# Last projection of a two-block transformer kernel: eight plain weight tiles against seven products with tokens as rows

## What is computed

```python
def second_block(x, ...):
    ...
        a = (a * jax.nn.silu(za)) @ w_att_out[l]
        ...
        sgo = (sgo * jax.nn.silu(zs)) @ w_sg_out[l]
        ga, gs = jnp.split(jax.nn.sigmoid(gm + b_merge[l]), N_BRANCHES, axis=-1)
        y = ga * a + gs * sgo
        x = x + y @ w_o[l]
    return rmsnorm_2(x, final_g)      # row mean of squares, 1/sqrt, times final_g
```

## Time and profile before

| what | us |
|---|---|
| median of 3 runs (1296.0 to 1296.04) | 1296.03 |
| the profiled execution's own time | 1295.99 |
| its span, from first to last recorded event | 1294.2 |
| TensorE busy (share of the span) | 1287.6 (99%) |
| VectorE busy | 818.7 (63%) |
| ScalarE busy | 622.6 (48%) |
| GpSimd busy | 703.7 (54%) |

### The profile page before, as it was taken

The page is one execution under the profiler, slowest core; times in us unless marked ns, Lnnn a source line. Parts: engine busy times, 40 slices in busy tenths (PEclk is TensorE's granted clock), DMA queues, the critical chain, the costliest instruction groups (busy, mean ns, idle before and its releaser), DMA issues.

```text
span 1294.2 us, 20065 instructions
## 1 busy us (share of the span) xinstructions
PE 1287.6 (99%) x7784; PEld 1116.6 (86%) x7784; DVE 818.7 (63%) x1253; ACT 622.6 (48%) x1004; POOL 703.7 (54%) x504
## 2 busy tenths in 40 slices
...
DMA packets 143626, 127.10 MB, mean 98 GB/s; under 512 B 4464, under 2 KB 138736, under 8 KB 143536
## 3 DMA queue, kind: packets, MB, share of 16 engines
...
## 4 chain that ended last, share of the span: by engine, by line
PE 99%; DMA 1%; ACT 0%; DVE 0%; issue 0%; SPq 0%; ACTq 0%
PE gemm L813 17%; PE gemm L814 17%; PE gemm L821 16%; PE gemm L1125 9%; PE gemm L1130 9%; PE gemm L1126 9%; PE gemm L870 2%; PE gemm L871 2%; PE gemm L876 2%; PE gemm L837 2%; PE gemm L838 2%; PE gemm L843 2%; PE mix L1251 1%; PE mix L1239 1%; PE mix L1228 1%; DMA xtm<-x 1%
## 5 line engine op out<-in xcount | busy, mean ns | idle before, releaser
L678 POOL TENSOR_TENSOR wlo<-raw,whi 128x512 fp32r<-128x512 f32 x280 | 388.2, 1419 | 307.3 <-ACT whi L1415 287.8
L813 PE MATMUL gemm<-hh,whi 128*128 128x512 f32 x584 | 232.1, 397 | 0.0
L814 PE MATMUL gemm<-hl,whi 128*128 128x512 f32 x584 | 227.8, 390 | 0.0
L706 POOL TENSOR_TENSOR wlo<-raw,whi 128x512 fp32r<-128x512 f32 x108 | 159.5, 1503 | 47.0 <-ACT whi L1624 41.6
L1415 ACT ACTIVATE whi<-raw 128x2048 fp32r<-128x2048 f32 x66 | 126.1, 1910 | 45.2 <-PE gemm L821 26.1
L821 PE MATMUL gemm<-hh,wlo 128*128 128x512 f32 x584 | 145.9, 390 | 0.0
L813 PEld LDWEIGHTS gemm<-hh,whi 128*128 128x128 f32 x584 | 109.7, 188 | 26.7 <-issue 4.0
L814 PEld LDWEIGHTS gemm<-hl,whi 128*128 128x128 f32 x584 | 109.8, 188 | 22.0 <-issue 0.2
L821 PEld LDWEIGHTS gemm<-hh,wlo 128*128 128x128 f32 x584 | 109.2, 188 | 22.4
L1125 PE MATMUL gemm<-hh,whi 128*128 128x256 f32 x496 | 124.7, 284 | 0.0
L1126 PE MATMUL gemm<-hl,whi 128*128 128x256 f32 x496 | 124.3, 283 | 0.0
...
## 6 DMA issues: line engine op xcount, KB each, us to landing
...
```

Source lines behind the costliest of these rows:

```text
L678: last = nc.gpsimd.tensor_tensor(a(wlo), a(raw), as_f32(a(whi)), ALU.subtract)
L706: return nc.gpsimd.tensor_tensor(part_of(wlo, u, b), raw_block(u, f, k), as_f32(part_of(whi, u, b)), sub)
L813: mm(bank[:, :], w, xh[:, k, :], start=(k == 0), stop=False)
L814: mm(bank[:, :], w, xl[:, k, :], start=False, stop=False)
```

## The change

The weights `w_o2` are cut into quadrants of 512 x 512: `wa[0]`, `wa[1]` are the upper k-half (feature columns 0 to 511 and 512 to 1023), `wb[0]`, `wb[1]` the lower. `y2` is cut into left and right tokens (256 each) and k-blocks 0 to 3 and 4 to 7. Seven quadrant products take the place of eight. In each, 128 tokens are the loaded operand and 512 weight columns stream, so results come out with tokens as rows and are added to rows of the residual, `xr[t]`. Those rows are made by 32 transposes of `xT` between the tiles of the `w_so` product, copied by ACT. The combinations are: sums of `y2` quadrants (`u_sum`, DVE), sums of weight quadrants (`w_sum` by DVE, `wa[1]` by POOL), their high parts (ACT) and rests (DVE, POOL), and sums of products afterwards. The order of products is P1, P2 (plain), P5, P6, P7 (of sums), P3, P4. Squares are summed along rows by ACT, and `fg2` becomes a broadcast row `fg2b`, loaded by DMA.

The diff, cut. Removed throughout are the units of `w_o2`, `turn_out`, `last_tile`, `turn_half`, `row_sum`, `last_rows`, `last_sum`, `square_out`, `copy_out` and the old `row_out`.

```diff
+sp.wait_ge(sem("mixed_ps"), KD)
+for f in range(2):
+    sp.dma_start(wa[f][:, :, :], cols(w_o2, f * 512, 512, 0, 4)).then_inc(sem("wT_in"), 16)
+for i, f in enumerate((1, 0)):
+    slot_free(n_o2 + i)
+    load(n_o2 + i, cols(w_o2, f * 512, 512, 4, 4), wb[f])
+sp.wait_ge(sem("y2_sum"), KD)
+sp.dma_start(fg2b[:, :], fg2_row.partition_broadcast(P)).then_inc(sem("c2_in"), 16)
+for t, h, done, count in ((2, 0, "out_dve", 1), (2, 1, "out_act", 1), (3, 0, "out_dve", 2), (3, 1, "out_act", 2),
+                          (0, 1, "out_dve", 3), (0, 0, "out_dve", 4), (1, 0, "out_act", 3), (1, 1, "out_dve", 5)):
+    sp.wait_ge(sem(done), count)
+    sp.dma_start(out[t * P:(t + 1) * P, h * 512:(h + 1) * 512], xr[t][:, h * 512:(h + 1) * 512]).then_inc(sem("o_out"), 16)
...
+def block_rest(i, block):
+    high, low = W_SLOT[LAST_SLOT[i]]
+    pool.wait_ge(sem("hi_done"), N_UNITS + i + 1)
+    for k in range(4):
+        last = nc.gpsimd.tensor_tensor(low[:, k, :], block[:, k, :], as_f32(high[:, k, :]), sub)
+    last.then_inc(sem("lo_done"), 1)
+block_rest(L_P1, wa[0])
+block_rest(L_P2, wb[0])
+pool.wait_ge(sem("s_made"), 3 * N_SEVEN + 1)
+for k in range(4):
+    last = nc.gpsimd.tensor_tensor(wa[1][:, k, :], wa[0][:, k, :], wa[1][:, k, :], sub)
+last.then_inc(sem("s3_made"), 1)
+pool.wait_ge(sem("o_copied"), 8)
+for t in range(2):
+    pool.wait_ge(sem("p1_read"), N_SEVEN + 1 + t)
+    o = xr[t][:, 0:512]
+    nc.gpsimd.tensor_tensor(o, o, p1_s(t), ALU.add).then_inc(sem("row_pre"), 1)
+block_rest(L_P7, wa[1])
+for t in range(2):
+    pool.wait_ge(sem("p1_read"), N_SEVEN + 3 + t)
+    o = xr[2 + t][:, 0:512]
+    nc.gpsimd.tensor_tensor(o, o, p5_s(t), ALU.add).then_inc(sem("row_pre"), 1)
+    pool.wait_ge(sem("row_pre"), 3 + 2 * t)
+    nc.gpsimd.tensor_tensor(p5_s(t), p5_s(t), xr[2 + t][:, 512:], ALU.add).then_inc(sem("row_pre"), 1)
+block_rest(L_P4, wb[1])
+pool.wait_ge(sem("c2_in"), 80)
+for t, h, count in ((2, 1, 3), (3, 1, 4), (1, 0, 2)):
+    pool.wait_ge(sem("row_sq"), count)
+    o = xr[t][:, h * 512:(h + 1) * 512]
+    nc.gpsimd.tensor_tensor(o, o, fg2b[:, h * 512:(h + 1) * 512], mult).then_inc(sem("row_pre"), 1)
...
+def turn_input(i):
+    t, h = TURNS[i]
+    if i == 0:
+        pe.wait_ge(sem("mixed"), KD)
+    if i >= 4:
+        pe.wait_ge(sem("o_copied"), i - 3)
+    for c in range(4):
+        last = nc.tensor.transpose(M[i % 4][:, c * P:(c + 1) * P], xT[:, 4 * h + c, t * P:(t + 1) * P], ident)
     last.then_inc(sem("o_ps"), 1)
+def turns_after(p, j):
+    if p < 3:
+        turn_input(2 * p + j)
+    elif j == 0:
+        turn_input(6)
+        turn_input(7)
+for p in range(4):
+    unit_fm(n_gs + 4 + p, sgh, sgl, after=lambda j: turns_after(p, j))
+def last_product(i, banks, xh, xl, low):
+    high, rest = W_SLOT[LAST_SLOT[i]]
+    pe.wait_ge(sem("hi_done"), N_UNITS + i + 1)
     for t in range(2):
+        tok = slice(t * P, (t + 1) * P)
+        for k in range(4):
+            mm(banks[t][:, :], xh[:, k, tok], high[:, k, :], start=(k == 0), stop=False)
+            mm(banks[t][:, :], xl[:, k, tok], high[:, k, :], start=False, stop=False)
+        if t == 0:
+            pe.wait_ge(sem(low[0]), low[1])
+        for k in range(4):
+            last = mm(banks[t][:, :], xh[:, k, tok], rest[:, k, :], start=False, stop=(k == 3))
+        last.then_inc(sem("last_ps"), 1)
+LOW, SUM_LOW = 2 * N_UNITS, 3 * N_SEVEN
+left, right = slice(0, HALF), slice(HALF, SEQ)
+pe.wait_ge(sem("o_copied"), 8)
+pe.wait_ge(sem("y2_lo"), 4)
+last_product(L_P1, B1, hh[:, 0:4, left], hl[:, 0:4, left], ("lo_done", LOW + 1))
+pe.wait_ge(sem("y2_lo"), KD)
+last_product(L_P2, B3, hh[:, 4:8, left], hl[:, 4:8, left], ("lo_done", LOW + 2))
+pe.wait_ge(sem("t_lo"), 12)
+last_product(L_P5, B2, u_hi[:, 0], u_lo[:, 0], ("s_lo", SUM_LOW + 1))
+pe.wait_ge(sem("t_lo"), 21)
+pe.wait_ge(sem("tile_free"), T_END)
+last_product(L_P6, B4, u_hi[:, 1], u_lo[:, 1], ("s_lo", SUM_LOW + 2))
+pe.wait_ge(sem("p1_read"), N_SEVEN + 2)
+last_product(L_P7, B1, u_hi[:, 2], u_lo[:, 2], ("lo_done", LOW + 3))
+pe.wait_ge(sem("p1_read"), N_SEVEN + 4)
+last_product(L_P3, B2, hh[:, 4:8, right], hl[:, 4:8, right], ("s_lo", SUM_LOW + 3))
+pe.wait_ge(sem("c_sum"), C_END + 2)
+last_product(L_P4, B3, hh[:, 0:4, right], hl[:, 0:4, right], ("lo_done", LOW + 4))
...
+act.preload_act_table_set(EXP_LN)
+def y2_high(m):
+    act.wait_ge(sem("y2_sum"), m + 1)
+    fn(y2h[:, m, kept(m)], y2[:, m, kept(m)], ACT.Copy).then_inc(sem("y2_hi"), 1)
+def keep_input(i):
+    t, h = TURNS[i]
+    act.wait_ge(sem("o_ps"), i + 1)
+    fn(xr[t][:, h * 512:(h + 1) * 512], M[i % 4][:, :], ACT.Copy).then_inc(sem("o_copied"), 1)
+def block_high(i, block):
+    fn(W_SLOT[LAST_SLOT[i]][0][:, :, :], block[:, :, :], ACT.Copy).then_inc(sem("hi_done"), 1)
+def sum_highs(g):
+    ks = K_GROUPS[g]
+    act.wait_ge(sem("t_made"), 8 + g)
+    fn(u_hi[:, 1, ks], u_sum[:, 1, ks], ACT.Copy).then_inc(sem("t_hi"), 1)
+    fn(u_hi[:, 2, ks], u_sum[:, 2, ks], ACT.Copy).then_inc(sem("t_hi"), 1)
+    fn(y2h[:, ks, HALF:], y2[:, ks, HALF:], ACT.Copy).then_inc(sem("t_hi"), 1)
+def keep_product(count, done, dst, banks, t):
+    act.wait_ge(sem("last_ps"), done + t)
+    fn(dst(t), banks[t][:, :], ACT.Copy).then_inc(sem("p1_read"), 1)
+squares = [0]
+def square_row(t, h, done):
+    act.wait_ge(sem("c_sum"), C_END + done)
+    if squares[0]:
+        act.wait_ge(sem("row_sq"), squares[0])
+    squares[0] += 1
+    fn(sq_junk[:, :], xr[t][:, h * 512:(h + 1) * 512], ACT.Square, accum_out=row_sq[:, t, h:h + 1]).then_inc(sem("row_sq"), 1)
+def row_root(t, h):
+    act.wait_ge(sem("row_b"), 1 if t < 2 else 2)
+    act.wait_ge(sem("row_sq"), squares[0])
+    link(fn(rcol[:, t:t + 1], row_sq[:, t, h:h + 1], ACT.Ln, scale=1.0 / DM, bias=row_b[:, t:t + 1]))
+    fn(rcol[:, t:t + 1], rcol[:, t:t + 1], ACT.Exp, scale=-0.5).then_inc(sem("R2"), 1)
+def row_out(t, h, root, pre):
+    act.wait_ge(sem("R2"), root)
+    act.wait_ge(sem("row_pre"), pre)
+    o = xr[t][:, h * 512:(h + 1) * 512]
+    fn(o, o, ACT.Copy, scale=rcol[:, t:t + 1]).then_inc(sem("out_act"), 1)
+keep_input(0)
+keep_input(1)
+y2_high(0)
+y2_high(1)
+keep_input(2)
+y2_high(2)
+keep_input(3)
+y2_high(3)
+act.wait_ge(sem("t_made"), 7)
+fn(u_hi[:, 0], u_sum[:, 0], ACT.Copy).then_inc(sem("t_hi"), 1)
+keep_input(4)
+y2_high(4)
+keep_input(5)
+act.wait_ge(sem("wT_in"), 48)
+act.wait_ge(sem("tile_done"), T_END - 2)
+block_high(L_P1, wa[0])
+y2_high(5)
+sum_highs(0)
+keep_input(6)
+keep_input(7)
+y2_high(6)
+sum_highs(1)
+act.wait_ge(sem(f"raw_in{(n_o2 + 1) % 2}"), raw_count(n_o2 + 1))
+act.wait_ge(sem("tile_done"), T_END)
+block_high(L_P2, wb[0])
+y2_high(7)
+act.wait_ge(sem("s_made"), 3 * N_SEVEN + 1)
+block_high(L_P5, w_sum)
+keep_product(1, 1, p1_s, B1, 0)
+sum_highs(2)
+keep_product(2, 1, p1_s, B1, 1)
+act.wait_ge(sem("s_made"), 3 * N_SEVEN + 2)
+block_high(L_P6, w_sum)
+act.wait_ge(sem("t_lo"), 21)
+keep_product(3, 5, p5_s, B2, 0)
+keep_product(4, 5, p5_s, B2, 1)
+act.wait_ge(sem("s3_made"), N_SEVEN + 1)
+act.wait_ge(sem("last_ps"), 2)
+block_high(L_P7, wa[1])
+square_row(0, 0, 1)
+square_row(1, 0, 2)
+act.wait_ge(sem("s_made"), 3 * N_SEVEN + 3)
+act.wait_ge(sem("last_ps"), 6)
+block_high(L_P3, w_sum)
+block_high(L_P4, wb[1])
+square_row(2, 1, 7)
+square_row(3, 1, 8)
+square_row(2, 0, 9)
+row_root(2, 0)
+square_row(3, 0, 10)
+row_root(3, 0)
+row_out(2, 1, 2, 7)
+square_row(0, 1, 11)
+row_root(0, 1)
+row_out(3, 1, 3, 8)
+square_row(1, 1, 12)
+row_root(1, 1)
+row_out(1, 0, 5, 9)
...
+def gated_rest(m):
+    tt(y2l[:, m, kept(m)], y2[:, m, kept(m)], as_f32(y2h[:, m, kept(m)]), ALU.subtract).then_inc(sem("y2_lo"), 1)
+def late_sums(g):
+    ks = K_GROUPS[g]
+    dve.wait_ge(sem("y2_sum"), 4 + ks.stop)
+    link(tt(u_sum[:, 2, ks], y2[:, later(ks), HALF:], y2[:, ks, HALF:], ALU.subtract))
+    link(tt(u_sum[:, 1, ks], u_sum[:, 2, ks], y2[:, ks, 0:HALF], ALU.add))
+    tt(y2[:, ks, HALF:], y2[:, later(ks), 0:HALF], u_sum[:, 1, ks], ALU.subtract).then_inc(sem("t_made"), 1)
+def late_rests(g):
+    ks = K_GROUPS[g]
+    dve.wait_ge(sem("t_hi"), 15 + 3 * g)
+    for i in (1, 2):
+        tt(u_lo[:, i, ks], u_sum[:, i, ks], as_f32(u_hi[:, i, ks]), ALU.subtract).then_inc(sem("t_lo"), 1)
+    tt(y2l[:, ks, HALF:], y2[:, ks, HALF:], as_f32(y2h[:, ks, HALF:]), ALU.subtract).then_inc(sem("t_lo"), 1)
+def block_sum(i, a, b, op):
+    if i:
+        dve.wait_ge(sem("s_lo"), 3 * N_SEVEN + i)
+    tt(w_sum[:, :, :], a[:, :, :], b[:, :, :], op).then_inc(sem("s_made"), 1)
+def block_rest(i):
+    high, low = W_SLOT[LAST_SLOT[i]]
+    dve.wait_ge(sem("hi_done"), N_UNITS + i + 1)
+    tt(low[:, :, :], w_sum[:, :, :], as_f32(high[:, :, :]), ALU.subtract).then_inc(sem("s_lo"), 1)
+for m in range(4):
+    gated_tile(m)
+    gated_rest(m)
+dve.wait_ge(sem("y2_sum"), 4)
+tt(u_sum[:, 0], y2[:, 0:4, HALF:], y2[:, 0:4, 0:HALF], ALU.subtract).then_inc(sem("t_made"), 1)
+dve.wait_ge(sem("t_hi"), 12)
+tt(u_lo[:, 0], u_sum[:, 0], as_f32(u_hi[:, 0]), ALU.subtract).then_inc(sem("t_lo"), 1)
+gated_tile(4)
+gated_rest(4)
```

(81 more changed lines are left out.)

204 lines of the change are left out of this document (25 added, 179 removed).

## The result

The changed kernel takes **1310.09 us** (median of 4 executions, 1309.89 to 1311.34) beside 1296.01 (4, 1295.96 to 1296.04) for the kernel before in the same session: ratio 1.0111, 95% interval 1.0093 to 1.0128. It is slower by 14.1 us; forecast were 1310.0 and +14.

The account below looks back on a forecast made before the run. TensorE, 99% busy, was taken to bound the kernel. Last product 1280.5 without waits, plus 17.6 of waits: 1298.1; tail 6.7, writes 3.5, execution 1.8 above span: 1310 us, +14; range 1296.5 to 1314.

Parts of the forecast that it names:

- TensorE's part: Last projection on TensorE: seven products of 38.1 us plus 3.5 us of transposes, so without waits it ends 6.8 us earlier.
- The seven waits: TensorE waiting for operands at P1, P2 (twice), P6 (twice), P7 and P4: 17.6 us in all.
- The price of 3.3 us for 2048 elements: A DVE instruction of 2048 elements with two SBUF inputs takes 3.3 us beside working POOL, 2.28 alone; used six times.
- the rule of whole instructions: DVE with two SBUF inputs and POOL exclude each other for a whole instruction, so a 2048-element one holds POOL throughout.
- DVE 90% busy from 1228 on: A sign that the forecast is right: DVE 90% busy from 1228 on the profile's time axis.
- The tail: From the last product's end to the last output instruction: 6.7 us, against 3.4 before.
- Rival A: DVE and POOL overlap freely, without turns; waits of 3.2 us, 1292 us in all, -4; chance 0.18.
- Rival B: 2048-element DVE instructions let POOL in midway, so the later waits vanish; 1297.3 us, +1.3; chance 0.15.
- Rival C: TensorE's granted clock falls to half after the wait before P2; up to 1313 us; chance 0.12.
- The bound of 3.2 us: Most that the fallen clock could cost, if all 24 of P2's instructions are slow: 5.4 - 2.2 us.

Follow-up runs that it names:

- rows without the sums: Changed kernel with tokens as rows and the early residual kept, but the last projection in eight plain quadrant products; 1294.54 us, ratio 0.9987.
- the run again: The changed kernel itself, unaltered, measured once more beside small edits of it; 1310.11 us, ratio 1.0107.
- fills as long as the subtractions: Changed kernel with each of POOL's 29 last-projection instructions replaced by two or three constant fills that read nothing, 1.36 us on average; 1296.17 us.
- plain ones: Changed kernel with each of POOL's 29 last-projection instructions replaced by one constant fill that reads nothing, 0.48 us; 1293.79 us, ratio 0.9982.
- the other order: Changed kernel with the first group's late rests after gated tile 6 on DVE, and the tail's combinations and outputs reordered; 1306.72 us, ratio 1.0080.

## Why the prediction was right

**TensorE's part, -6.8.** Right. The row form costs next to nothing: rows without the sums end within 0.6 us of where their instructions at 0.2267 us put them.

**The seven waits, 17.6.** Right point by point, within 0.35 us, where the clock doesn't blur it. Starts as predicted, and in the run with TensorE kept busy: P1 1243.9 and 1244.24; P2 1254.05 and 1254.40; its rest 1258.1 and 1258.37; P6 1269.4 and 1269.54; its rest 1272.7 and 1272.83; P7's rest 1281.8 and 1281.95; P4's 1294.4 and 1294.46. The gaps shown add up to less than 17.6, because each is counted from the end of a pipelined instruction (0.39 us long, 0.2267 apart), 0.16 us short each time, and because the changed kernel's slow stretches filled some. Its own gaps, 11.3 us, would be a wrong reading of the cost: the other 5 us are TensorE at half clock, all but the last 1 us of it over waits that were due.

**The price of 3.3 us for 2048 elements.** Right, as the price of the pair. Of the five with POOL at work DVE took 3.36, 3.26 and 3.37; in the two beside P7's rests it took 2.28 and 2.27, and POOL waited, up to 3.45 us for one instruction of 512 (3.3 was said). The trace of before had nothing longer than 1024; the rule of whole instructions, on which that price was worked on, holds at 2048. "DVE 90% busy from 1228 on" came out as 84% (60.7 of 72 us), partly because POOL did that waiting.

**The tail, 6.7.** 6.5 measured. The waits and the tail may be added up only because the tail was followed along DVE's queue, in which the outputs of rows 2 and 3 stand ahead of the sum for rows 0 (until 1299.75 predicted, 1299.5 in the run again, on the same axis). To read the sum as "TensorE is late, so all is late" would be wrong for the end: its last product was over 3 us early.

**Rival A** put the kernel without turns at 1292; fills as long as the subtractions gave 1296.2, plain ones 1293.8. The mechanism is the one that decides, its size was off by 4.2 us, and the earlier trace rows had already ruled the rival out for two inputs in SBUF. The chance of 0.18 was too high for what those rows show. **Rival B** (turns given back midway) is refuted by the 9.4 us of POOL's four. **Rival C**: the clock fell, in P2 as said and in P7, which I had left out; it returned 4 to 8 us after TensorE had resumed, and cost 0.1 us in the median, because a wait or DVE's queue lay behind each, and 0.7 in the profiled execution. The bound of 3.2 us took no account of the waits further down.

**My expectation for the other order failed by 2.6 us.** It took the last product at 3 us earlier and the tail at 3 us shorter. The tail did get 3.4 shorter; the last product gained 0.8, since the lead was 2.3 and the clock fell behind the wait ahead of the last rests (1.5 us), and the crowded writes took 0.8 back. Turns that fall differently from execution to execution were left out too (1.0 us between the two profiled ones, in a spread of 2.4).
